# All RWKV projections of a layer in one piece ahead of the attention, through a DRAM scratch: a two-layer hybrid encoder step on Trainium2

## What is computed

```
P  = h @ w_in                       # columns: q 512 | k 128 | v 128 | r 512 | k 512 | v 512 | w 64 | a 64 | g 160
q, ka, va -> rotary, sliding-window attention with sinks          (group A, 8 heads, 2 kv heads)
pr = P[..., 768:]
p_prev = concat([shift0, pr[:, :-1]]);  ps = pr + (p_prev - pr) * mu     # token shift
r, k, v, xw, xa, xg = split(ps)
w_raw = -softplus(-(w0 + tanh(xw) @ w2)) - 0.5;  decay = exp(-exp(w_raw))
a = sigmoid(a0 + xa @ a2);  g = sigmoid(xg) @ g2
kk = normalise(k * k_k);  k_f = k * (1 + (a - 1) * k_a)
for t:  S = S*decay_t + (S @ -kk_t) (kk_t a_t)^T + v_t k_f_t^T;  y_t = S r_t       # 8 heads of 64
out = concat([attn, (groupnorm(y) + bonus) * g]) @ w_out;   last row of pr is an output too
```

## Time and profile before

| | |
|---|---|
| median of three runs | 5038.05 us (5037.1 to 5039.85) |
| the profiled execution | 5030.11 us, span 5028.5 us |
| TensorE busy, mean granted clock | 3913.9 us, 0.846 of 2.4 GHz |
| VectorE, ScalarE, GpSimd busy | 1932.6, 1427.0, 336.3 us |

### The profile page before, as it was taken

How to read it: one execution, slowest core, us unless ns; L and a number is a source line. 1 busy time by engine, 2 the same in 40 slices (tenths; PEclk the granted TensorE clock), 3 DMA queues, 4 the chain that set the end, 5 groups by cost and what they waited for, 6 DMA issues and landing times. The chain is left out here.

```text
span 5028.5 us, 90738 instructions
## 1 busy us (share of the span) xinstructions
PE 3913.9 (78%) x32444; PEld 3592.6 (71%) x32444; DVE 1932.6 (38%) x3243; ACT 1427.0 (28%) x2837; POOL 336.3 (7%) x470
## 2 busy tenths in 40 slices
PE   4976677776676799999658767776767668999995
PEld 3955666666665699999657556665557567999994
DVE  3243443443243433333442533434432425333334
ACT  3233232331234311112242331332323343111113
POOL 0010111111000000000000101112110000000000
PEclk7967877887788899999878777877778888999997
DMA  4100000000210011111121000000002100111111
GB/s 165 32 19 15 11 20 3 20 24 2 99 34 17 26 47 46 46 42 50 33 94 34 13 20 3 20 17 6 23 11 103 34 17 26 42 50 46 46 46 47
DMA packets 211172, 182.19 MB, mean 36 GB/s; under 512 B 17524, under 2 KB 194884, under 8 KB 210080
## 3 DMA queue, kind: packets, MB, share of 16 engines
q1 hardware_dynamic: 199392, 128.60, 8.6%
q0 software_dynamic: 11456, 49.32, 2.5%
HBM read 152.23 MB, written 25.65 MB: 35 GB/s over the span
## 5 line engine op out<-in xcount | busy, mean ns | idle before, releaser
L583 PE MATMUL PS<-HH,WH 128*128 128x352 f32 (+1 forms) x3680 | 1205.3, 328 | 89.8 <-PEq L567 89.8
L583 PE MATMUL PS<-HH,WL 128*128 128x352 f32 (+1 forms) x3680 | 1190.0, 323 | 0.0
L583 PE MATMUL PS<-HL,WH 128*128 128x352 f32 (+1 forms) x3680 | 1188.4, 323 | 0.0
L583 PEld LDWEIGHTS PS<-HH,WH 128*128 128x128 f32 x3680 | 704.1, 191 | 109.2 <-issue 106.0
L583 PEld LDWEIGHTS PS<-HH,WL 128*128 128x128 f32 x3680 | 705.4, 192 | 0.8
L583 PEld LDWEIGHTS PS<-HL,WH 128*128 128x128 f32 x3680 | 702.9, 191 | 0.0
L1130 ACT COPY R<-PS 128x128 f32<-128x128 f32 (+9 forms) x843 | 291.1, 349 | 1316.3 <-ACTq L1143 577.4
L1708 DVE TENSOR_TENSOR WL<-WRAW,WH 128x1024 fp32r<-128x1024 f32 x226 | 293.2, 1297 | 867.3 <-DVEq L1707 867.3
L1130 ACT CAST WH<-WRAW 128x1024 fp32r<-128x1024 f32 x234 | 245.5, 1049 | 611.6 <-ACTq L1135 611.6
L574 PE MATMUL PS<-CST,R 128*128 128x128 f32 (+3 forms) x944 | 174.4, 347 | 273.1 <-PEq L567 273.0
L574 PEld LDWEIGHTS PS<-CST,R 128*128 128x128 f32 (+3 forms) x944 | 142.0, 180 | 306.5 <-issue 302.6
(11 more groups left out here) (250 smaller groups left out, 5496.9 us busy)
## 6 DMA issues: line engine op xcount, KB each, us to landing
WRAW<-in_w_gate_up SPq DMA_DIRECT2D x88, 512.0 KB, 3.7
WRAW<-in_w_down SPq DMA_DIRECT2D x46, 512.0 KB, 3.2
WRAW<-in_w_in SPq DMA_DIRECT2D x38, 512.0 KB, 3.7
x_spill<-R POOLq DMA_DIRECT2D x2, 4224.0 KB, 12.8
R<-mix_dram POOLq DMA_DIRECT2D x16, 528.0 KB, 6.8
R<-x_spill POOLq DMA_DIRECT2D x2, 4224.0 KB, 20.0
WRAW<-in_w_mem_kv SPq DMA_DIRECT2D x16, 512.0 KB, 3.7
WRAW<-in_w_out SPq DMA_DIRECT2D x16, 512.0 KB, 3.7
```

The lines of the kernel that those rows point to most:

```text
L583: ins = e.matmul(out, lhs(k, wp), rhs(k, xp), start=first, stop=(k == n - 1 and xp == 1))
```

## The change

All twelve blocks of r, k and v join the three lora blocks in one piece of 15 (`BLOCKS`) ahead of the attention. They use PSUM banks 0 to 5 in turn. `PRAW` becomes two buffers `PR` that lie with two `SHIFTED` rows beside `HH` and `HL`, where `GH` and `GL` of the SwiGLU are later. VectorE's `shifted(n)` first makes the low half of the weights of block n + 2 and then shifts block n; a row of r, k or v goes by SyncE to the DRAM scratch `rkv_dram`. SyncE's order is load n, then store n - 2. The two last loads of the piece are the first blocks of `w_out`. In a pair, SyncE loads the lora weights straight into `LW` (now over a row of `HL`) and the rows k, r and v, once ScalarE gives `rows_free`: after the attention, and in each pair after its last outputs. The three dense blocks, their copies, casts, low halves and shifts leave the pair.

In the attention the tile loops of TensorE, VectorE and ScalarE are written out, ScalarE's order in a tile is by_key 0, exps 0, by_key 1, exps 1, weighted 0, weighted 1, values, the values pass through bank 0 in place of 7, and tanh and the sigmoids (`lora_gates`) come behind the eighth tile. GpSimd loads cos and sin at once. Some semaphores of the cross-attention share a name with ones of the attention.

SyncE:

```
-            w8(1, io["w_in"], l, R0 + 3 * R_WIDTH)
-            w8(0, io["w_in"], l, R0 + 3 * R_WIDTH + P)
...
+            for n in range(BLOCKS + 2):
+                block_in(n)
+                if n >= 5:
+                    block_out(n - 2)
             with e.Fori(0, PAIRS) as j:
-                w8(0, io["w_in"], l, j * P + R0)
-                e.wait_ge(S("w_free1"), 1)
-                lw = WRAW[:, 1, :]
...
-                for b in range(1, 3):
-                    w8(b - 1, io["w_in"], l, j * P + R0 + b * R_WIDTH)
-            stream(io["w_out"], l, 4)
+                e.wait_ge(S("rows_free"), 1)
...
+                for dst, src in parts:
+                    e.dma_start(dst, src.rearrange("a r n -> (a r) n")[:, bass.ds(j * P, P)]).then_inc(S("lw_full"), 16)
+                for b, dst, name in ((1, KF, "row_k"), (0, RR, "row_r"), (2, VV, "row_v")):
+                    e.dma_start(dst, rkv_dram[bass.ds(j + b * PAIRS, 1)].rearrange("a p t -> (a p) t")).then_inc(S(name), 16)
+            stream(io["w_out"], l, 3, 2 * P)
```

TensorE (`proj(k)` is chunk k % 3 of block k // 3, 24 matmuls; `BLOCKS` is 15):

```
-            for n in range(8):
+            for n in range(5):
                 dense8(n % 2, 3 * (n % 2), "dense_psum")
+            for k in range(CH * BLOCKS):
+                proj(k)
```

TensorE, in the pair:

```
-                dense8(0, 0, "dense_psum")
-                e.wait_ge(S("lw_ready"), 1)
+                e.wait_ge(S("lw_full"), 64)
...
-                dense8(0, 0, "dense_psum")
-                dense8(1, 3, "dense_psum", chunks=(0, 1))
...
-                dense8(1, 3, "dense_psum", chunks=(2,), first=False)
```

ScalarE, `proj(k)`: wait for `praw_free`, copy the chunk to `PR[n % 2]`, free the bank; after the third chunk:

```
+                    give(e, "praw_ready")
+                    split(block_slot(n))
```

ScalarE, in the attention tile:

```
-                for g in range(2):
-                    by_key(g, P, (P, P))
-                for g in range(2):
-                    if not last:
-                        exps(g, P, 256)
-                    weighted(g, P)
+                by_key(0, P, (P, P))
+                exps(0, P, 256)
+                by_key(1, P, (P, P))
+                exps(1, P, 256)
+                weighted(0, P)
+                weighted(1, P)
```

VectorE, in the piece at the head:

```
+            def shifted(n):
+                m, praw, at = block_rows(n), PR[n % 2], 12 + n if n < 3 else n - 3
+                dst = (TWA, SG1, SG2[0:32, :])[n] if n < 3 else SHIFTED[n % 2]
+                lo(block_slot(n))
...
+                give(e, f"praw_free{n % 2}")
+                if n == 2:
+                    give(e, "lora_ready")
+                elif n > 2:
+                    give(e, "shifted_ready")
+            for n in range(BLOCKS):
+                shifted(n)
```

VectorE, in the pair:

```
-                e.tensor_copy(LW, WRAW[:, 1, 0:3 * P]).then_inc(S("dve_done"), 1)
...
-                row(0, RR)
-                lo(0)
...
-                lo(1)
-                row(1, KF)
+                e.wait_ge(S("row_k"), 16)
...
-                lo(0)
-                row(2, VV)
```

More of the change, by code:

```diff
@@ L333, in _, with block_in @@
-            stream(io["w_out"], l, 4)
+            def block_in(n):
+                if n == 2:
+                    weight(block_slot(n), w_block(io["w_in"], l, R0 + 3 * R_WIDTH + 2 * P, 32),
+                           view=lambda d: d.rearrange("p (k n) -> p k n", k=DB)[:, :, 0:32])
+                elif n < BLOCKS:
+                    w8(block_slot(n), io["w_in"], l, R0 + (3 * R_WIDTH + n * P if n < 2 else (n - 3) * P))
+                else:
+                    w8(block_slot(n), io["w_out"], l, (n - BLOCKS) * P)
@@ L733, in _, with tile @@
             both = [(0, 256, 0)]
-            def tile(i, last):
-                if not last:
-                    swapped(i, P)
-                for g in range(2):
-                    by_key(g, P, both)
-                    if not last:
-                        scores(g, P, both)
-                for g in range(2):
-                    weighted(g, P, both)
-                if not last:
-                    values(P)
+            def tile(t):
+                i = t * P
+                swapped(i, P)
+                by_key(0, P, both)
+                scores(0, P, both)
+                by_key(1, P, both)
+                scores(1, P, both)
+                weighted(0, P, both)
+                weighted(1, P, both)
+                values(P)
             swapped(0, P)
@@ L751, in _ @@
             values(P)
-            with e.Fori(0, TILES - 1) as i:
-                tile(i * P + P, False)
-            tile(None, True)
+            for t in range(1, TILES):
+                tile(t)
+            for g in range(2):
+                by_key(g, P, both)
+            for g in range(2):
+                weighted(g, P, both)
             keys_out(P, 1)
@@ L1334, in keys_out, with tile @@
                 give(e, "bank0", "ko_ready")
[L1336 to L1340, removed]
-                    by_key(g, P, (P, P))
-                for g in range(2):
-                    if not last:
-                        exps(g, P, 256)
-                    weighted(g, P)
-                if not last:
-                    values(P, slot)
+            def tile(t):
+                value_stage(t * P, P)
+                by_key(0, P, (P, P))
[4 more added lines that the diff above has]
+                weighted(1, P)
+                values(P, t % 2)
             value_stage(0, P)
-            values(P, 0)
             exps(0, P, 256)
             exps(1, P, 256)
[L1353 to L1356, removed]
-            tile(None, None, True)
+            values(P, 0)
+            for t in range(1, TILES):
+                tile(t)
+            for g in range(2):
+                by_key(g, P, (P, P))
+            for g in range(2):
+                weighted(g, P)
+            lora_gates()
             keys_out(P)
@@ L1376, in _ @@
             barrier(e, "act")
+            give(e, "rows_free")
             def by_token(u):
@@ L1953, in _, with tile @@
             e.sem_inc(S("dve_done"), -1)
-            def tile(i, slot, mask, last):
+            def tile(t):
+                mask = odd if t % 2 else even(t // 2)
                 normalised(0, P, 256)
-                if not last:
-                    rotary(i, P, slot)
+                rotary(t * P, P, t % 2)
                 normalised(1, P, 256)
-                if not last:
-                    masked(0, P, 256, mask)
-                    masked(1, P, 256, mask)
-            even = lambda i: CST[:, bass.ds(C_AE + i * 256, 256)]
+                masked(0, P, 256, mask)
+                masked(1, P, 256, mask)
+            even = lambda i: CST[:, C_AE + i * 256:C_AE + (i + 1) * 256]
             odd = CST[:, C_AO:C_AO + 256]
@@ L1969, in _ @@
             masked(1, P, 256, even(0))
-            with e.Fori(0, TILES // 2 - 1) as i:
-                tile((i * 2 + 1) * P, 1, odd, False)
-                tile((i * 2 + 2) * P, 0, even(i + 1), False)
-            tile(SEQ - P, 1, odd, False)
-            tile(None, None, None, True)
+            for t in range(1, TILES):
+                tile(t)
+            normalised(0, P, 256)
+            normalised(1, P, 256)
             e.wait_ge(S("kc_ready"), 1)
```

189 lines of the change are left out of this document (107 added, 82 removed).

## The result

The changed kernel takes 5248.41 us (median of four runs, 5240.11 to 5251.77) against 5037.58 us of the kernel before, measured beside it (5033.38 to 5039.85). The ratio is 1.0417, with an interval of 1.0399 to 1.0435: slower by 211 us. The forecast was 5280 us, with a range of 5190 to 5335. The profiled execution took 5240.11 us, its span 5238.6, which is 210.1 more than the span before.

A forecast was written before the change was run, and what follows sets the result against it. TensorE bounds the head's projections; a ring of waits over four engines bounds attention tiles and RWKV pairs. Per layer 137.4 + 17 - 4.4 + 43 + 6.1 - 78 = +121, two layers +242: 5280 us, range 5190 to 5335.

The forecast's parts named there:

- Blocks into the head: Projections ahead of the attention: twelve more blocks at 11.45 us of TensorE time each, +137.4 us per layer.
- The ring on SyncE: Head: loads queued behind stores of shifted rows make a round 13.0 us against TensorE's 11.45, +17 us per layer.
- The rival of a slack ring: Head: load and store overlap fully, so TensorE sets the pace, 34 us less, 5246 us; chance 0.17.
- that of 14.4 us a round: Head: loads land after 5.8 us and more, slower rounds, 30 us more, 5310 us; chance 0.18.
- End of the head: Ahead of the first rotary swap: shorter wait -3.1 us, gates' table load gone -1.3, together -4.4 per layer.
- Attention tiles: Attention: by_key 1 waits behind exps 0, delaying the second masking multiply; 6.1 us a tile, seven tiles, +43 per layer.
- The rival that the token does not bind: Attention: the score buffer's second token costs nothing, attention stays as it is, 86 us less, 5194; chance 0.1.
- Gates: ScalarE between the last weighted copy and keys_out: tanh and sigmoids +4.8 us, exponentials' table +1.3, together +6.1.
- Front of a pair: RWKV pair, last YY multiply to the units' release: steps taken out sum to -17.9 us for pairs 1 to 3.
- Units unchanged: RWKV pair behind the release: the units start at the half clock as before, so no term was given.
- fronts of pair 0: First RWKV pair, with no tail to load in: sigmoid earlier, then the same 14.7 us, together -24.3.
- The rival on the other side: RWKV fronts: TensorE's queue paces them, 36 us a pair comes out, 5025 us, faster than before; chance 0.02.

The follow-up runs named there:

- e1_ring: The changed kernel with SyncE storing shifted row n-3 behind load n instead of row n-2; 5203.8 us, ratio 1.0331 to the kernel before.
- e8_cos: The kernel before with the raw row buffer moved off the memory of cos and sin, so both load at once; 5017.7 us, ratio 0.9957.
- e2_order: The changed kernel with ScalarE's old attention tile order put back, loops still written out and values in bank 0; 5163.8 us, ratio 1.0247.
- e4_light: The kernel before with each pair's three dense blocks cut from 72 matmuls to one per chunk, all else kept; 4972.1 us, ratio 0.9869.
- e3_mended: The changed kernel with SyncE storing row n-3, ScalarE's old tile order, and the lora gates back ahead of the attention; 5110.6 us, ratio 1.0141.
- e12_lo: The kernel before with VectorE's third weight subtraction of each pair moved from ahead of v's shift to behind the bonus products; 5020.5 us, ratio 0.9955.

## Why the prediction was right, and where it was off

The direction, the size and the order of the terms held; 211 us were measured where 242 were forecast. That the total came so near is in part luck: terms that were off by some 51 us one way and by some 20 the other are added up in it (below).

- **Blocks into the head**, 11.45 us each: right. With the ring opened (e1_ring) the rounds are 11.44.
- **The ring on SyncE**, 13.0 us a round, 17 us a layer: measured 13.13, and 19.4 when taken out. The term of 4.4 us from issue to landing was 4.2, which gives 12.8 for the usual round; two rounds of the eleven took 14.3, and in the second layer three took 14.0 to 14.1. The rival of a slack ring is refuted, and that of 14.4 us a round holds for these few rounds alone. The forecast quoted the Trainium skill, "DMA: Bandwidth & Descriptors", section "Anatomy of one DMA", whose figures are for transfers that GpSimd issues; the estimate of 4.4 us from them is near the 4.2 us that SyncE's loads took here, and no run tests the rule itself.
- **End of the head**, -3.1: the first swap comes 153.0 us later; less 137.4 and the ring's 19.4 that is -3.8. e8_cos shows that cos alone gives -5.9, so some 2 us came back in the changed kernel in some other way; which was not tested.
- **Attention tiles**, +43: without the gates the attention is 41.1 and 36.8 us longer, and e2_order takes out 38.9 in each layer by the traces (42 by the medians). The delay of the masking multiply was forecast at 2.2 us and is 2.1. The rival that the token does not bind is refuted.
- **Gates**, +6.1: measured 6.6 (39.0 against 32.4).
- **Front of a pair**, -17.9: measured -15.6, mean of six, and -15.8 in pair 1. Its later steps were right (pair 1): sigmoid table load to square -8.7 forecast (scan and square) and -8.5 measured, square to Ln -1.8 and -1.9 (the forecast's terms add up to 6.25 us and not to its 6.4; 6.26 was measured), Ln to memset -4.2 and -4.3. The step that failed is the first, the sigmoid table load 3.2 us sooner: it came 1.0 sooner (7.48 us after the YY multiply before, 6.46 now), because VectorE's copy of the bias column (867.20), for which ScalarE waits, has 1.87 us of idle time ahead of it that no semaphore explains. All six fronts have it (1.87 to 2.19 us). What that is stays open.
- **Units unchanged**: this step was wrong. They do start at the half clock as before, as the text said, but the clock granted later is higher (0.80 instead of 0.73 over the units), and they are 5.0 us shorter each, 40 us in all. The forecast put this term at nothing because it looked at the start of the units alone. The 32 us by which the forecast was too high, as measured minus forecast: units -40, fronts of pairs 1 to 3 +14, fronts of pair 0 -6, head +6, attention -5.
- **The rival on the other side** (TensorE's blocks pace the front, worth 36 us a pair) is refuted by e4_light: they are worth 0.5 us there, and 4.2 more by way of the clock.

The change then costs, per layer, 137.4 us for blocks that were free in pairs 1 to 3, some 65 us of waits that it makes itself (19.4, 38.9 and 6.6), and gets back 4 us at the end of the head and 90 to 98 us in the pairs. That is handling by ScalarE and VectorE and a better clock; of TensorE's own time only pair 0 gives some back (12 to 15 us in e4_light). Even with its own waits mended (e3_mended) it is 1.4% behind.

## What to carry to other kernels

Matmuls in a stretch that another chain sets cost next to nothing there (0.5 us a front) and their full time in a stretch that TensorE sets (11.45 us a block). Before moving them, cut them out where they stand and look whether that stretch gets shorter, and the next one too: here the clock of the stretch behind was worth 4.2 us. When a queue issues loads and stores by turns, ask for each store what it waits for and which load stands behind it. A freed or reordered copy on ScalarE is worth what its token lets start, so follow the token, not the copy.

## What the runs showed of the hardware

TensorE's work in one stretch lowered the clock that it was granted in a later one. With 84 more matmuls in the front and under the tail before it, and with 9 more in the front, the units behind were 8.2 and 5.7 us longer. In the first 30 us of the units the clock was no lower than in the changed kernel; most of the loss came from 50 us on (the table's last columns). 33 us of blocks less made the units 4.2 us shorter. And VectorE's subtraction of 128x1024 took 3.30 us beside GpSimd's products of 128x1056, in all eight pairs, and 1.22 without them (e12_lo).
